# Idle turns of the identity in the last expert's waits, in the first projection and ahead of the affinities; sums of squares behind the projection

## What is computed

```
def expert_choice_ffn(h, w_router, w1, w3, w2):
    aff = jax.nn.softmax((h @ w_router).astype(jnp.float32), axis=-1)
    gate, idx = lax.top_k(jnp.swapaxes(aff, 1, 2), cap)
    xe = jax.vmap(lambda hb, ib: hb[ib])(h, idx)
    hid = jax.nn.silu(jnp.einsum('becd,edf->becf', xe, w1)) * jnp.einsum('becd,edf->becf', xe, w3)
    ye = jnp.einsum('becf,efd->becd', hid, w2) * gate[..., None].astype(h.dtype)
...
def mla_swa_layer(x, positions, g_in, w_in, g_q_a, w_q_up, g_kv_a, w_kv_up, sinks, w_out):
    h = rms_norm(x, g_in)
    z = h @ w_in
    cq, ckv, kpe, q_s, k_s, v_s, gate = split_cols(z, EVEN_SPLITS)
```

## Time and profile before

| | |
|---|---|
| median of 3 runs | 1394.73 us (1394.66 to 1395.79) |
| profiled execution, its own time | 1392.89 us |
| its span | 1391.1 us |
| mean granted clock of TensorE | 0.861 |
| TensorE busy, products | 990.3 us (71%) |
| VectorE busy | 403.7 us (29%) |
| ScalarE busy | 239.6 us (17%) |
| GpSimd busy | 81.3 us (6%) |
| moved | 482.47 MB, mean 347 GB/s |

### The profile page before, as it was taken

How to read it: one execution, slowest core, us unless ns; L and a number is a source line. 1 busy time by engine, 2 the same in 40 slices (tenths; PEclk the granted TensorE clock), 3 DMA queues, 4 the chain that set the end, 5 groups by cost and what they waited for, 6 DMA issues and landing times.

```text
span 1391.1 us, 15269 instructions
## 1 busy us (share of the span) xinstructions
PE 990.3 (71%) x6645; PEld 509.5 (37%) x6645; DVE 403.7 (29%) x972; ACT 239.6 (17%) x482; POOL 81.3 (6%) x74
## 2 busy tenths in 40 slices
PE   5998987666666655656765655555656789899987
PEld 3855832212211111111111111111111688799875
DVE  4866411011011110101001010110101467775584
ACT  3535110000000000000000000000000345643452
POOL 1300000000020000000000000000000043200020
PEclk9999999879886888888768688888878799999999
DMA  9995889999999999999999999999999343144311
GB/s 397 388 379 221 344 364 429 426 428 428 426 427 428 428 428 428 427 428 428 428 426 429 428 428 429 427 427 428 426 427 429 153 160 122 61 182 158 145 61 46
DMA packets 34771, 482.47 MB, mean 347 GB/s; under 512 B 3854, under 2 KB 3856, under 8 KB 5520
## 3 DMA queue, kind: packets, MB, share of 16 engines
q1 hardware_dynamic: 34240, 479.92, 82.5%
q10 hardware_dynamic: 288, 1.05, 0.2%
q0 software_dynamic: 176, 0.53, 0.1%
HBM read 480.43 MB, written 1.05 MB: 346 GB/s over the span
## 4 chain that ended last, share of the span: by engine, by line
DMA 57%; PE 32%; DVE 6%; ACT 3%; issue 1%; SPq 0%; POOL 0%; POOLq 0%; DVEq 0%; ACTq 0%
DMA ring<-in_t_w 55%; PE PS L500 7%; PE PS L488 6%; PE PS L998 6%; PE PS L1044 2%; DMA ring<-in_t_mod 2%; ACT S L613 2%; PE PS L679 1%; PE PS L477 1%; PE PS L580 1%; PE PS L986 1%; PE PS L775 1%; PE PS L797 1%; DVE S L594 1%; PE PS L913 1%
## 5 line engine op out<-in xcount | busy, mean ns | idle before, releaser
L998 PE MATMUL PS<-ring,S 128*32 128x512 f32 x2016 | 321.5, 771 | 217.9 <-DMA ring<-in_t_w 215.3
L1044 PE MATMUL PS<-ring,S 128*32 128x512 f32 x1008 | 170.1, 809 | 106.7 <-DMA ring<-in_t_w 97.9
L998 PEld LDWEIGHTS PS<-ring,S 128*32 128x32 f32 x2016 | 62.8, 126 | 456.0 <-DMA ring<-in_t_w 338.5
L506 DVE COPY S<-PS 128x512 f32<-128x512 f32 (+2 forms) x47 | 32.1, 683 | 310.7 <-PE PS L1044 291.6
L500 PE MATMUL PS<-SR,RR 128*128 128x256 f32 x736 | 117.4, 285 | 1.2 <-DVE ab L1424 0.9
L1044 PEld LDWEIGHTS PS<-ring,S 128*32 128x32 f32 x1008 | 33.1, 128 | 225.8 <-DMA ring<-in_t_w 151.3
L500 PEld LDWEIGHTS PS<-SR,RR 128*128 128x128 f32 x736 | 103.7, 189 | 2.6 <-DVE ab L1424 1.2
L452 ACT ACTIVATE RR<-ring 128x1024 fp32r<-128x1024 f32 (+3 forms) x95 | 89.3, 1000 | 39.4 <-DMA ring<-in_t_e_a 18.2
L1540 DVE TENSOR_SCALAR S<-PS,KC 128x256 f32<-128x256 f32 x16 | 7.7, 484 | 277.9 <-PE PS L1028 277.9
L458 DVE TENSOR_TENSOR RR<-ring,RR 128x1024 fp32r<-128x1024 f32 (+2 forms) x76 | 84.2, 1156 | 8.5 <-ACT RR L452 8.5
L488 PE MATMUL PS<-RR,SR 128*128 128x512 f32 (+4 forms) x296 | 83.3, 393 | 3.8 <-DVE S L523 3.8
(11 more groups left out here) (305 smaller groups left out, 982.3 us busy)
## 6 DMA issues: line engine op xcount, KB each, us to landing
ring<-in_t_w SPq DMA_DIRECT2D x189, 2048.0 KB, 31.4
ring<-in_t_mod SPq DMA_DIRECT2D x12, 2048.0 KB, 12.9
ring<-in_t_out SPq DMA_DIRECT2D x6, 2048.0 KB, 7.8
S<-in_t_w SPq DMA_DIRECT2D x3, 2048.0 KB, 12.3
ring<-in_t_e_g SPq DMA_DIRECT2D x2, 2048.0 KB, 8.3
ring<-in_t_o_q SPq DMA_DIRECT2D x2, 2048.0 KB, 7.9
ring<-in_t_o_k SPq DMA_DIRECT2D x2, 2048.0 KB, 8.5
ring<-in_t_o_v SPq DMA_DIRECT2D x2, 2048.0 KB, 8.2
```

The costliest lines, as they stand in the source:

```text
L506: lane.e.tensor_copy(dst, src).then_inc(*lane.mark(out_of(key), *names))
L998: m = pe.e.matmul(PS[32 * j:32 * j + 32, b, :], expert_rows(2 * k + kk, e_, e_ + 1), place[name, e_, k][:, kk, 512 * j:512 * j + 512], sta ...
L1044: m = pe.e.matmul(PS[q:q + 32, b, :], HT[e_ % 2][:, 128 * s + 32 * j:128 * s + 32 * j + 32], place["w2", e_, j][:, s, 512 * dh:512 * dh + ...
```

## The change

A helper `awake(key, group, number)` takes a bank and puts that many transposes of the identity there. It is called ahead of "affT" (12 turns) and behind it (24, where 36 stood); in the last expert ahead of the second, third and fourth block of w2 (16 each, bank 6) and ahead of the last scatter (6, bank 6); in the first projection behind its second, fourth and sixth group of three products (6 each, bank 7). The sums of squares, which stood among the groups of the first projection, go behind the second one. `spread_rows` goes behind both halves of "qst". On VectorE a second piece of the weights of "qst" goes ahead of the wait for the sums.

```
+        def awake(key, group, number):
+
+            b = banks.take(key, group)
+            pe.wait_ge(banks.was[key])
+            for n in range(number):
+                m = pe.e.transpose(PS[:, b, 128 * (n % 4):128 * (n % 4) + 128], ident, ident)
+            m.then_inc(*pe.mark(out_of(key)))
...
         x1_back(1)
+        awake(("awake", 0), ALL6, 12)
         b = banks.take("affT", ALL6)
...
-        for n in range(36):
-            m = pe.e.transpose(PS[:, b, 128 * (n % 4):128 * (n % 4) + 128], ident, ident)
-        m.then_inc(*pe.mark(out_of("awake")))
+        awake("awake", ALL6, 24)
...
             for j in range(4):
+                if e_ == E - 1 and j:
+                    awake(("awake", j), (6,), 16)
                 pe.wait_ge(("load", ("w2", e_, j)))
...
+        awake(("awake", 4), (6,), 6)
         scatter(E - 1)
...
-            if n >= 2:
-                c, dh = KORD[n - 2] % 4, KORD[n - 2] // 4
-                pe.wait_ge(("sqs", c), "gg", *[banks.was["ss", i] for i in range(2)])
-                for i in range(2):
-                    m = pe.e.matmul(PS[:, banks.of["ss", i], 0:2], sqs[:, c, 256 * dh + 128 * i:256 * dh + 128 * i + 128],
-                                    gg[:, KORD[n - 2], :], start=n == 2, stop=n == len(KORD) + 1)
+            if n == len(KORD) - 1:
+                m.then_inc(*pe.mark(("za", 0)))
+            elif n % 2:
+                awake(("awake", "za", n), (7,), 6)
+        project(pe, ("za", 1), ("e", "a"), HE, 1, 416, ks=KORD, final=True)
+        pe.wait_ge("gg", *[("sqs", c) for c in range(4)], *[banks.was["ss", i] for i in range(2)])
+        for i in range(2):
+            for k in KORD:
+                m = pe.e.matmul(PS[:, banks.of["ss", i], 0:2], sqs[:, k % 4, 256 * (k // 4) + 128 * i:256 * (k // 4) + 128 * i + 128],
+                                gg[:, k, :], start=k == KORD[0], stop=k == KORD[-1])
         m.then_inc(*pe.mark("ss"))
-        project(pe, ("za", 1), ("e", "a"), HE, 1, 416, ks=KORD, final=True)
...
         for n2 in range(2):
             straight(pe, ("qst", n2), ("e", "qs"), HE, n2, final=n2 == 1)
-            if n2 == 0:
-                spread_rows("e", 4)
+        spread_rows("e", 4)
...
-        lo_piece(dve, ("e", "qs"), 0)
+        for c in (0, 2):
+            lo_piece(dve, ("e", "qs"), c)
         dve.wait_ge("ss")
...
-        for c in (2, 4, 6):
+        for c in (4, 6):
             lo_piece(dve, ("e", "qs"), c)
```

More of the change, by code:

```diff
@@ L963, in pe_program @@
         m.then_inc(*pe.mark("affT"))
-        b = banks.take("awake", ALL6)
-        pe.wait_ge(banks.was["awake"])
-        for n in range(36):
-            m = pe.e.transpose(PS[:, b, 128 * (n % 4):128 * (n % 4) + 128], ident, ident)
-        m.then_inc(*pe.mark(out_of("awake")))
+        awake("awake", ALL6, 24)
         b = banks.take("post", ALL6)
@@ L1055, in pe_program @@
         pe.wait_ge(banks.was["za", 0])
[L1056 to L1070 removed]
+        for n, k in enumerate(KORD):
+            pe.wait_ge(("split", ("e", "a"), k), ("he", k))
+            for m_, (l_, r_) in enumerate(products(("e", "a"), HE, k, slice(0, 416), slice(0, 128))):
+                m = pe.e.matmul(PS[:, banks.of["za", 0], 0:416], l_, r_, start=(n == 0 and m_ == 0),
+                                stop=(n == len(KORD) - 1 and m_ == 2))
+            if n == len(KORD) - 1:
[8 more added lines that the diff above has]
+                                gg[:, k, :], start=k == KORD[0], stop=k == KORD[-1])
         m.then_inc(*pe.mark("ss"))
[L1072 removed]
         def spread_rows(name, n):
```

9 lines of the change are left out of this document (removed).

## The result

The changed kernel takes **1405.26 us** (median of 6 runs, 1401.72 to 1407.68); the kernel before, run on the same chip, 1394.70 (6 runs, 1392.32 to 1398.95). The ratio is 1.0067, 95% interval 1.0051 to 1.0083: slower by 7 to 12 us. The forecast was 1399.2 us, with a range up to 1402.8: the direction was right, and the time lies 2.5 us above the range. The profiled execution took 1403.27 us, its span is 1401.4; the span before was 1391.1.

A forecast was written before the change was run, and what follows sets the result against it. The experts' weight stream on the DMA bounds the middle, the engines set the pace before and behind it. Terms 1.9 - 0.5 + 0 + 2.3 + 1.2 = +4.9 us on 1392.89; forecast 1399.2 us, range 1392.4 to 1402.8.

The forecast's parts named there:

- Router: Turns around the affinities: positions' transposes start 0.9 us earlier, the gather loses 2.8 us to a fallen clock; sum +1.9 us.
- Last expert: Turns in its waits: last block 1.92 us in place of 3.46, gain limited by the first projection's weight load; -0.5 us.
- First projection: Turns wait for bank 7 until 1096.7, then unbroken work, partly at half clock, ends at 1113.0 as before; 0, bounds -2.3 and +9.
- Straight projection: L500 behind the sums: late weight pieces +0.7 us, half clock after two-column products about +1.6; +2.3 us, bounds +0.7 and +4.
- The rows that spread the norm: L1079 behind the second half: copy, one piece and its subtraction come uncovered ahead of L1094; +1.2 us, bounds +0.8 and +2.
- A: Rival: clock held through gather and projections, bank 7's wait costs little; -1.3 us, 1393.4 us, no change; chance 0.17.
- D: Rival: clock returns early in the first projection and holds to 1125; end 3 to 4 us earlier, 1391.0 us; chance 0.13.
- C: Rival: turns don't hold the clock, so they overrun the last expert's gaps, projection at half; about +9, 1403.7 us; chance 0.03.

The follow-up runs named there:

- sums_block: Kernel before with the sums of squares as one block behind both projections, VectorE's second lo piece earlier, no new turns, rows between the halves: 1395.0 us, ratio 0.9989.
- router_left: Changed kernel with the rows back between the halves and the projection's turns in a free bank, its router kept (12 turns ahead, 24 behind): 1395.15 us, ratio 1.0001.
- last_turns: Kernel before with only the turns in the last expert's waits and ahead of the last scatter added: 1394.25 us, ratio 0.9992.
- rows_late: Kernel before with only the rows that spread the norm moved behind both halves of the straight projection: 1402.07 us, ratio 1.0041.
- rows_back: Changed kernel with the rows that spread the norm put back between the two halves of the straight projection: 1401.48 us, ratio 1.0039.
- out_first: Changed kernel with VectorE's read of the straight projection's first half (L1605) ahead of the four lo pieces of the next weights: 1404.52 us, ratio 1.0060.
- bank_only: Changed kernel with the rows back between the halves and the old router (36 turns behind), the projection's turns still in bank 7: 1397.4 us, ratio 1.0020.
- router_only: Kernel before with only the router's turns changed, 12 ahead of the affinities and 24 behind where 36 stood behind: 1396.85 us, ratio 1.0004.

## Why the prediction was right or wrong

- **Router, +1.9** (bounds -0.9 and +2.8). In the profile +2.65 at the queue, near the upper bound: -0.7 for the earlier start and +3.3 for a gather wholly at half clock. In the other traces Q-R is 21.5 to 23.0 against 20.1 to 20.6, so +1 to +2.9 (sums_block and router_left left out, for the reason above). That the stream hands it on is shown (B-Q). In times it was not resolved, neither alone nor undone; whether something behind gives it back, or the runs are too few, stays open.
- **Last expert, -0.5.** The last block took 1.92 us as forecast. VectorE's first L458 came at 1091.12, which is 0.9 earlier against its weights than before (1089.58, weights 1087.75). In last_turns the last block is as short. That 0.5 us reach the end is not shown: the interval of last_turns takes in zero, and in the changed kernel's profile S-B is 29.3 where it was 29.2.
- **First projection, 0.** The wait for bank 7 was foreseen with its releaser (L1535) and its end within what the stream added, and S-B is 29.3 as before. The unbroken stretch from the turns on took 16.4 us (1099.05 to 1115.48), and 14.0 + 2.3 had been summed for it. It was still a price: with a free bank S-B is 24.4 to 26.4. The block of sums seems to have paid for the wait (S-B 25.0 in sums_block), though one trace of a kernel is weak evidence for this column. The bound of 25.6 us all at half clock is right with 4.2 us for the 18 turns (18 x 0.231), not with the 3.9 printed.
- **Straight projection, +2.3.** +1.45 in the profile, +1.8 to +2.8 in the five other traces with the sums in a block and the rows behind both halves (13.26 to 14.23 us for the 96 products). The 0.7 us for late pieces did not come: in the changed kernel no piece held it up. What it measured is the clock at half behind the two-column products, as argued; rows_late, without their block, has 11.48.
- **The rows that spread the norm, +1.2** (bounds +0.8 and +2). This is the step that failed. That the move uncovers a wait ahead of kst was right; which path ends that wait was wrong, and the clock behind it was put at nothing. It measured 3.75 us of wait and 2.5 of clock, **+6.2**. The prediction followed kst's weights: the rows' copy, one piece and its subtraction. That path was priced well, for the first piece is done 1.2 us into the wait. But kst's bank has a tenant, the tenant's reader (L1605) stands behind all four pieces in VectorE's program, and this path ends 2.5 us later. And behind a TensorE idle for 3.7 us the 24 products ran at half clock. rows_late shows the whole term without the rest of the change, wait, clock and time (median +6.4). rows_back takes wait and clock away, for 3.8 us of time. out_first shows which path it was: with the reader moved ahead, 1.58 us are left, and they belong to the weights.

With 6.2 in place of 1.2 the sum is 1.9 - 0.5 + 0 + 2.3 + 6.2 = 9.9, and 1392.89 + 9.9 + 1.84 = 1404.6 against 1405.26 measured. Some of that closeness is luck: in the profile the first three terms came to 2.5 and not 1.4, and the fourth to 1.45 and not 2.3, which nearly cancel. The prices of the parts by medians are rows 6.4, bank 2.5, and the others each 0 within 2 to 3 us. They are not additive: rows_back is 6.0 over before with bank and router left in it, where bank_only has 2.5 and router_only 1.4. That excess of 2 us is not explained, nor that rows_back gives back 3.8 of the 6.4 us that rows_late costs.

Of the rivals, A and D needed the clock held through the gather or the projection; both places lost it. C needed turns that don't hold the clock. They held it over the last expert's waits (1.00 from 1071.9 to 1090.9), and with the turns alone (last_turns) all four blocks take 1.92 us too. The Trainium skill (TensorE: Matmul & The Clock Gate, Part 4: PE-mode transpose) says that full clock does not engage for transposes; the changed kernel's trace disagrees, as the one before did.

## What to carry to other kernels

Before a read is moved later, look up the tenant of each buffer or bank that the work behind it will take, and what stands ahead of the tenant's last reader in that reader's program; the wait is the whole queue, not the next instruction. Price an idle TensorE twice, once as the wait and once as the products behind it at half clock: here 3.7 us of waiting cost 1.6 to 2.7 us more. When a wait is shortened, look at what the work that now comes earlier meets on the other engines: here an expected gain of 2.3 to 4.8 us came out as 0.8, and a collision with GpSimd took a good part of the rest.

## What the runs showed of the hardware

- VectorE multiplies of 128x32 with both operands in SBUF took 2.37 us beside GpSimd pieces of 2.4 us and 0.18 without. The additions L523 of 128x80 are hit the same way: 2.37 to 2.39 us beside a piece, also in the kernel before, and 0.23 without.
- The same gather of 32 products of 32 columns took 3.73 us in all seven traces in which 36 turns ended just ahead of it, and 5.6 to 7.0 in the ten others, one with 46 turns among them. Why is open.
- kst's group behind a wait of 3.74 us took 4.46 to 5.49 us in five traces; behind 1.58 us, twice, 3.0 and 3.1; without a wait 2.83 to 2.88.
- One kernel's executions differ by up to 11 us (router_only: 1390.44 to 1401.67); in the shortest the clock stood at 1.00 from 1097.6 to 1138.9.
